# The first weights of seven projections fetched and split in the last turn of the stage before

## The reference

```python
for layer in range(DEPTH):
    h = rmsnorm(x, norm_mix[layer]) * (1 + sc1) + sh1           # both token groups
    y = hyena_mlstm_mixer(...) if layer % 2 == 0 else mla_mixer(...)
    x = x + g1 * y
    x = x + g2 * conv_ffn(rmsnorm(x, norm_ffn[layer]) * (1 + sc2) + sh2, *ffn_p[layer])
x = rmsnorm(x, final_norm)
# second block: one input projection, split by columns
q, k, v, z, xbc, dt_raw, gates = jnp.split(rmsnorm_2(x, norm_mix_w) @ w_in, split_at, axis=-1)
merged = g_attn * (attention @ w_attn_o) + g_ssd * (state_space(z, xbc) @ w_ssd_o)
x = x + merged @ w_out
x = x + hierarchical_moe(rmsnorm_2(x, norm_ffn_w))
```

## Time and profile before

| | |
|---|---|
| median of 3 timed runs | 3491.16 us (3490.48 to 3492.16) |
| the profiled execution | 3485.01 us, span of its instructions 3483.2 us |
| TensorE busy | 3002.3 us, 86% |
| VectorE, ScalarE busy | 1699.8 us (49%), 1214.2 us (35%) |
| mean granted TensorE clock | 0.927 |

### The profile page before, as it was taken

The page is one execution under the profiler, slowest core; times in us unless marked ns, Lnnn a source line. Parts: engine busy times, 40 slices in busy tenths (PEclk is TensorE's granted clock), DMA queues, the critical chain, the costliest instruction groups (busy, mean ns, idle before and its releaser), DMA issues. The chain is left out here.

```text
span 3483.2 us, 38114 instructions
## 1 busy us (share of the span) xinstructions
PE 3002.3 (86%) x14263; PEld 2349.5 (67%) x14263; DVE 1699.8 (49%) x2349; ACT 1214.2 (35%) x1614; POOL 164.8 (5%) x131
## 2 busy tenths in 40 slices
PE   6896788978999999978999999978857788499996
PEld 2382367767888887756777887857635566477775
DVE  1343332354576643424564443341366554488886
ACT  0220022233323232423333442233323322377774
POOL 0000000110001100000000000000000100221210
PEclk9997899899999999989999999989978898699998
DMA  6311011011235333101002221212200013399996
GB/s 244 113 48 64 19 49 49 1 37 73 92 122 169 113 123 100 67 19 45 7 2 96 97 96 68 89 43 85 72 7 1 1 49 146 140 350 350 343 339 241
DMA packets 76311, 362.79 MB, mean 104 GB/s; under 512 B 13428, under 2 KB 17347, under 8 KB 50596
## 3 DMA queue, kind: packets, MB, share of 16 engines
q1 hardware_dynamic: 62404, 327.69, 26.6%
q0 software_dynamic: 13792, 33.58, 2.8%
HBM read 360.68 MB, written 16.27 MB: 108 GB/s over the span
## 5 line engine op out<-in xcount | busy, mean ns | idle before, releaser
L288 PE MATMUL ps<-rounded,rounded 128*128 128x512 f32 (+3 forms) x3700 | 1374.0, 371 | 108.7 <-DVE rounded L1978 24.1
L289 PE MATMUL ps<-rounded,rounded 128*128 128x512 f32 (+3 forms) x3700 | 1334.6, 361 | 0.0
L290 PE MATMUL ps<-rounded,rounded 128*128 128x512 f32 (+3 forms) x3700 | 1332.9, 360 | 0.0
L288 PEld LDWEIGHTS ps<-rounded,rounded 128*128 128x128 f32 (+1 forms) x3700 | 703.8, 190 | 284.8 <-issue 69.5
L290 PEld LDWEIGHTS ps<-rounded,rounded 128*128 128x128 f32 (+1 forms) x3700 | 704.1, 190 | 107.3
L289 PEld LDWEIGHTS ps<-rounded,rounded 128*128 128x128 f32 (+1 forms) x3700 | 705.7, 191 | 95.0
L267 DVE TENSOR_TENSOR rounded<-work,rounded 128x1024 fp32r<-128x1024 f32 (+3 forms) x224 | 306.4, 1370 | 817.5 <-ACT rounded L263 817.0
L263 ACT CAST rounded<-work 128x1024 fp32r<-128x1024 f32 (+3 forms) x224 | 260.8, 1166 | 701.2 <-PE ps L290 561.9
L3125 DVE TENSOR_TENSOR rounded<-work,rounded 128x2048 fp32r<-128x2048 f32 x138 | 311.7, 2288 | 91.1 <-ACT rounded L2973 88.5
L2973 ACT CAST rounded<-work 128x2048 fp32r<-128x2048 f32 x138 | 258.6, 1909 | 83.6 <-PE ps L290 83.6
L274 PE MATMUL ps<-cst 128*128 128x256 f32 x544 | 157.8, 455 | 105.2 <-PEq L169 105.2
(11 more groups left out here) (435 smaller groups left out, 2587.3 us busy)
## 6 DMA issues: line engine op xcount, KB each, us to landing
work<-in_moe SPq DMA_DIRECT2D x138, 1024.0 KB, 7.3
work<-in_ffn_up SPq DMA_DIRECT2D x44, 1024.0 KB, 4.8
work<-in_ffn_down SPq DMA_DIRECT2D x66, 512.0 KB, 3.5
work<-in_ada_w SPq DMA_DIRECT2D x12, 2048.0 KB, 8.6
work<-in_ada_w POOLq DMA_DIRECT2D x48, 512.0 KB, 4.1
work<-in_w_out SPq DMA_DIRECT2D x16, 512.0 KB, 3.5
work<-in_w_gates SPq DMA_DIRECT2D x16, 512.0 KB, 3.6
work<-in_w_in_hy SPq DMA_DIRECT2D x12, 512.0 KB, 3.3
```

What stands on the lines that cost most here:

```text
L288: k.nc.tensor.matmul(out, sh, mh, start=start, stop=False)
L289: k.nc.tensor.matmul(out, sh, ml, start=False, stop=False)
L290: return k.nc.tensor.matmul(out, sl, mh, start=False, stop=stop)
```

## The change

A `Stream` can be made `ahead` of its stage. It then uses one of two sets of semaphores that are not cleared between stages, with a `base` that counts what earlier streams on the set have added. The stage before gets it as `then`: SP issues its first two loads behind its own (`begin`), ScalarE casts tile p right behind the last product that reads slot p and ahead of its evacuation, VectorE subtracts, and the stage itself leaves these steps out. ffn_down's streams get `places` of their own, inside ffn_up's: both raw tiles in ffn_up's raw slot 0, the parts in its raw slot 1 and in the high part of its slot 0. The dummy products at the start of these seven stages go. Seven streams are made ahead: og, ffn_down of block 0 twice and of block 1 once, z, gates, xbc. All other streams pass through the same code with base 0. Left out below are the rest of `project_conv` (SP and VectorE as in `ffn_down` and `ffn_up`, and the dummies only where the stream is not ahead) and `project_act`, edited alike, with `then.low` for both tiles at the end of VectorE's program.

```diff
@@ -235,35 +237,50 @@
 class Stream:
-    def __init__(self, k, name, width, n=2):
-        self.k, self.src, self.n = k, k.dram[name], n
+
+
+    def __init__(self, k, name, width, n=2, ahead=False, places=None):
+        self.k, self.src, self.n, self.ahead = k, k.dram[name], n, ahead
         self.tiles = self.src.shape[0]
         at = MEM - 3 * n * width
         self.at = at - WORK_AT
-        self.raw = [k.words(at + s * width, at + (s + 1) * width) for s in range(n)]
-        spots = [(at + (n + 2 * s) * width, at + (n + 2 * s + 1) * width) for s in range(n)]
+        raw, spots = places or ([at + s * width for s in range(n)],
+                                [(at + (n + 2 * s) * width, at + (n + 2 * s + 1) * width) for s in range(n)])
+        self.raw = [k.words(a, a + width) for a in raw]
         self.parts = [tuple(k.rounded_words(a, a + width) for a in spot) for spot in spots]
         self.high_plain = [high.bitcast(F32) for high, low in self.parts]
-        self.landed, self.rounded, self.ready = ([k.sem(f"{w}{s}") for s in range(n)] for w in ("landed", "rounded", "ready"))
+        self.base = 0
+        if ahead:
+            self.base = sum(other.tiles // n for other in k.ahead[len(k.ahead) % 2::2])
+            self.landed, self.rounded, self.ready = k.ahead_sems[len(k.ahead) % 2]
+            k.ahead.append(self)
+        else:
+            self.landed, self.rounded, self.ready = ([k.sem(f"{w}{s}") for s in range(n)] for w in ("landed", "rounded", "ready"))
         assert self.tiles % n == 0
-    def load(self, sp):
+    def begin(self, sp, before=None):
         for s in range(self.n):
+            if before:
+                sp.wait_ge(before.ready[s], before.base + before.tiles // before.n)
             sp.dma_start(self.raw[s], self.src[s]).then_inc(self.landed[s], 16)
+
+    def load(self, sp, begun=False):
+        if not self.ahead and not begun:
+            self.begin(sp)
         if self.tiles > self.n:
             with sp.Fori(1, self.tiles // self.n) as i:
                 for s in range(self.n):
-                    sp.wait_ge(self.ready[s], i)
+                    sp.wait_ge(self.ready[s], i + self.base)
                     sp.dma_start(self.raw[s], self.src[i * self.n + s]).then_inc(self.landed[s], 16)
     def high(self, act, s, loads):
-        act.wait_ge(self.landed[s], 16 * loads)
+        act.wait_ge(self.landed[s], 16 * loads + 16 * self.base)
         self.k.nc.scalar.copy(self.parts[s][0], self.raw[s]).then_inc(self.rounded[s], 1)
     def low(self, dve, s, loads):
-        dve.wait_ge(self.rounded[s], loads)
+        dve.wait_ge(self.rounded[s], loads + self.base)
         self.k.nc.vector.tensor_tensor(self.parts[s][1], self.raw[s], self.high_plain[s],
                                        ALU.subtract).then_inc(self.ready[s], 1)
@@ -761,6 +780,8 @@
                     act.wait_ge(product[p], i + 1)
                     if not last:
                         stream.high(act, p, i + 2)
+                    elif then:
+                        then.high(act, p, 1)
                     bias = k.col(conv_b, n) if conv_b else 0.0
                     nc.scalar.activation(sums(n, p), k.pair(p)[:, t0:T], ACT.Identity,
                                          scale=k.col(conv_w, n + tiles * (taps // 2)), bias=bias).then_inc(middle, 1)
@@ -823,6 +846,8 @@
         @block.sync
         def _(sp):
             stream.load(sp)
+            sp.wait_ge(stream.ready[0], turns)
+            then.begin(sp)
         @block.tensor
         def _(pe):
@@ -857,6 +882,9 @@
                     act.wait_ge(product[p], i + 1)
                     if not last:
                         stream.high(act, p, i + 2)
+                    else:
+                        act.wait_ge(stream.ready[1], turns)
+                        then.high(act, p, 1)
                     act.wait_ge(taken[p], i + 1)
                     for a, w in segs:
@@ -887,6 +915,8 @@
                     n = 2 * i + p
                     if kind != "last":
                         stream.low(dve, p, i + 2)
+                    else:
+                        then.low(dve, p, 1)
                     dve.wait_ge(middle, ns * (n + 1))
                     for a, w in segs:
                         out = scratch[:, p, a + 1:a + w]
@@ -931,13 +961,14 @@
         @block.sync
         def _(sp):
             stream.load(sp)
+            if then:
+                then.begin(sp, stream)
         @block.tensor
         def _(pe):
-            keep_running(k)
             def turn(i, first, last):
                 for p in range(2):
-                    pe.wait_ge(stream.ready[p], i + 1)
+                    pe.wait_ge(stream.ready[p], i + (stream.base + 1))
                     pe.wait_ge(cut, 2 * i + p + 1)
                     for n in range(DT):
                         done = three_passes(k, k.bank(n, w), [part[:, n * P:(n + 1) * P] for part in stream.parts[p]],
@@ -952,7 +983,8 @@
         @block.scalar
         def _(act):
             def high(n, p, loads):
-                stream.high(act, p, loads)
+                if loads > 1:
+                    stream.high(act, p, loads)
                 nc.scalar.copy(inner.high[:, p, 0:w], hidden[:, n, t0:t0 + w]).then_inc(rounded, 1)
             for p in range(2):
@@ -961,11 +993,16 @@
                 for p in range(2):
                     act.wait_ge(product[p], i + 1)
                     high(2 * i + p + 2, p, i + 2)
+            if then:
+                for p in range(2):
+                    act.wait_ge(product[p], turns)
+                    then.high(act, p, 1)
         @block.vector
         def _(dve):
             def low(n, p, loads):
-                stream.low(dve, p, loads)
+                if loads > 1:
+                    stream.low(dve, p, loads)
                 dve.wait_ge(rounded, n + 1)
                 nc.vector.tensor_tensor(inner.low[:, p, 0:w], hidden[:, n, t0:t0 + w], inner.high_plain[:, p, 0:w],
                                         ALU.subtract).then_inc(cut, 1)
@@ -1378,8 +1425,9 @@
 def mlstm(k, mixed):
     q, key, og = k.area(8 * T, 4, T), k.area(12 * T, 4, T), k.area(16 * T + 6 * 516, 4, T)
     v = k.arena[:, 16 * T:16 * T + 6 * 516].rearrange("p (c h n) -> p c h n", h=ML_HEADS, n=P + 1)
-    project_conv(k, "w_in_qk", k.area(8 * T, 8, T), "ml_conv_w", None, True)
-    project_act(k, "w_in_og", og, ACT.Sigmoid, None, SEGS)
+    w_og = Stream(k, "w_in_og", D, ahead=True)
+    project_conv(k, "w_in_qk", k.area(8 * T, 8, T), "ml_conv_w", None, True, then=w_og)
+    project_act(k, w_og, og, ACT.Sigmoid, None, SEGS)
     project_tokens(k, "w_in_v", v[:, :, :, 0:P], DT, k.h_pair, range(6), ML_W)
     mlstm_core(k, q, key, v, og, k.area(0, 4, T), mixed)
@@ -2615,10 +2663,11 @@
     probs = [k.words(WORK_AT + b * LAT, WORK_AT + (b + 1) * LAT).rearrange("p (c t) -> p c t", t=LAT)
              for b in range(2)]
     load(k, ((cos, "rope_cos"), (sin, "rope_sin")))
-    project_act(k, "w_qk_2", qk, ACT.Identity, None, SEG_LAT, norm=norm)
-    project_act(k, "w_z_2", z, ACT.Silu, None, SEG_LAT)
-    project_act(k, "w_gates_2", gates, ACT.Sigmoid, "b_gate_2", SEG_LAT)
-    project_conv(k, "w_xbc_2", xbc, "conv_w_2", "conv_b_2", True, 7, SEG_LAT)
+    w_z, w_gates, w_xbc = (Stream(k, name, D, ahead=True) for name in ("w_z_2", "w_gates_2", "w_xbc_2"))
+    project_act(k, "w_qk_2", qk, ACT.Identity, None, SEG_LAT, norm=norm, then=w_z)
+    project_act(k, w_z, z, ACT.Silu, None, SEG_LAT, then=w_gates)
+    project_act(k, w_gates, gates, ACT.Sigmoid, "b_gate_2", SEG_LAT, then=w_xbc)
+    project_conv(k, w_xbc, xbc, "conv_w_2", "conv_b_2", True, 7, SEG_LAT)
     project_values(k, v, steps)
     ring = [k.ring[:, j * LAT:(j + 1) * LAT] for j in range(4)]
     normalise_heads(k, qk, lambda n: k.col("qk_norm_2", 0 if n < 4 else 1), ring[0:2], ring[2:4])
@@ -3170,6 +3219,15 @@
     with ExitStack() as ctx:
         k = Kernel(nc, ctx, dram)
+        def ffn(layer, mod, norm, segs, **more):
+
+            at, half = MEM - 6 * 2 * D, 2 * D
+            places = [at, at + D], [(at + half, at + half + D), (at + 2 * half, at + 2 * half + D)]
+            down = [Stream(k, f"ffn_down_{layer}", D, ahead=True, places=places) for seg in segs]
+            ffn_up(k, layer, hidden, scratch, segs, norm, down[0], **more)
+            for n, seg in enumerate(segs):
+                ffn_down(k, down[n], hidden, mod, seg, down[n + 1] if n + 1 < len(segs) else None)
+
         def gain(a):
             return lambda kk, c: k.gain[:, a, kk, c:c + 1]
```

More of the change, by code:

```diff
@@ L732, in _ @@
                 norm.sum_and_spread(pe)
-            else:
+            elif not stream.ahead:
                 keep_running(k)
@@ L752, in _ @@
                 norm.square(act)
-            for p in range(2):
+            for p in range(0 if stream.ahead else 2):
                 stream.high(act, p, 1)
```

49 lines of the change are left out of this document (30 added, 19 removed).

## The result

The changed kernel took 3475.16 us (median of five), the kernel before 3492.16 us in the same comparison: 17 us less. The forecast was 3464.8 us, range 3457 to 3473: the sign is right, the time is 2 us outside the range. Two later comparisons of the same two kernels gave 0.9931 and 0.9914. The 14 runs of the changed kernel have a median of 3470.7 us (3460.7 to 3477.9). The 35 runs of before that stand beside them, on the same three chips, have one of 3493.0: **22.3 us less**, which the expectation of e10 had at 20 to 26.

A forecast was written before the change was run, and what follows sets the result against it. TensorE was taken to set the pace, except at seven starts bound by weight fetch and split. 32.5 - 6.7 - 0.6 + 1.2 = 26.4 us off the profiled 3485.0, plus 6 us for timed runs, gave 3464.8 us, range 3457 to 3473.

The forecast's parts named there:

- Starts, 32.5 us: At the seven stage starts: 48.32 us, minus what cannot be moved, minus lateness from splits in the stage before, saves 32.5 us.
- The lateness of TensorE's first instruction: At og, z, gates and xbc: TensorE's first instruction was assumed 0.05 us after SP's.
- Clock given back, -6.7 - 0.6 + 1.2: Without dummies, og, latent and block 1 lose 6.7 us, the context half 0.6; z wins 1.2, gates and xbc nothing.
- cold starts: At og and the three ffn_down, first real products run at 1.2 GHz, at double length for 3.5 to 5.5 us.
- The rival of the clock that holds: At z, gates and xbc: no low stretch, giving 6.3 instead of 1.2 us, so 3459.7 us; chance 0.17.
- The step that failed is the last one: Whole kernel: 26.4 us off the profiled 3485.0 us, then the same 6 us up to timed runs, giving 3464.8 us.
- The range: Whole kernel: own range 3461 to 3470 us; the clock that holds lowers it to 3457, longer tails raise it to 3473.
- levels of the clock behind later waits: Reason given for the range: these levels fall otherwise when everything is shifted; no size given.
- What would make it wrong: First products waiting for a DMA, a barrier over 3 us later, or stretches outside the seven changing by over 3 us.
- Slower, by the clock: In ffn_down's latent halves TensorE does not regain 2.4 GHz without dummies; 3705 us if both stay at 1.2; chance 0.02.

The follow-up runs named there:

- e10: The changed kernel once more, unchanged, against the kernel before on the same chip: 3467.78 us, ratio 0.9914.
- e8: The fill: changed kernel with dummy products behind the last product of the stage before, except ahead of block 0's latent ffn_down half: 3462.11 us, ratio 0.9894.
- e9: e8 plus dummies around the value projections ahead of block 1's attention (12 instead of 8 at the start, 5 behind the last product): 3450.39 us, ratio 0.9875.
- e15: The same kernel as e9 once more, for its profile and to confirm the time: 3456.55 us, ratio 0.9902 to before.
- e14: Changed kernel with dummies only around the value projections (12 instead of 8 at the start, 5 behind the last product), a repeat: 3462.78 us, ratio 0.9916.
- e6: Changed kernel with only z, gates and xbc begun ahead; og and the three ffn_down start as before, with dummies: 3480.76 us, ratio 0.9945.
- e4: Kernel before with only the dummy products of the seven starts left out, nothing made ahead: 3499.52 us, ratio 1.0027.
- e7: Changed kernel with only og and the three ffn_down begun ahead; z, gates and xbc start as before, with dummies: 3485.86 us, ratio 0.9963.
- e11: The kernel before once more, unchanged, for its profile: 3499.52 us (one run).

## Why the prediction was wrong in its number and right in its parts

- *Starts, 32.5 us*: 32.54 measured. The lateness of TensorE's first instruction was 0.1 to 0.2 us more than assumed at z, gates and xbc (4.92, 5.62 and 5.69 saved, against 5.09, 5.79 and 5.77), made up at the three ffn_down (4.41, 3.09 and 4.11 against 4.27, 2.85 and 3.97).
- *Clock given back, -6.7 - 0.6 + 1.2*: by stretch, means of three profiles of each kernel. Block 0's qk to values 119.24 to 115.08, 4.2 us gained (forecast 3.0); its feed-forward 624.76 to 619.67, 5.1 (3.9); block 1's 418.84 to 419.00, a loss of 0.2 (gain of 1.6); block 2's 248.40 to 230.42, 18.0 (17.9). Sum 27.0 against 26.4. By all seven profiles with these starts it is 3.5, 3.9, 0.5 and 18.1, sum 26.0. That the sums meet so closely is in part luck: of the 4.2 us, 1.0 is chance, as two of the three profiles of before have 3.4 us at 1.2 GHz at the start of qk itself and none of after's has, and the low lengths behind og and the latent half were mis-sized by 1.1 and 1.4 us in opposite directions. That cold starts cost about what was set down is shown by the fill: the clock behind the starts is 1.00, and the stretches are 4.1 us shorter in e8 and 7.3 us on average over e8, e9 and e15. The rival of the clock that holds came true at one start of the three, at gates in after and at xbc in e14 and e6.
- *The step that failed is the last one*: "The timed runs lie 6 us above it, at 3491.2; the same difference gives 3464.8 us". It takes 26.4 us off the median of three timed runs and so puts every change of the clock outside the seven starts at nothing. The runs show that this term is not small: with no edit at all the rest of the span is 2068.8, 2081.6 and 2087.9 us in the three profiles of before, and 2083.4 to 2090.2 in those of after, and single runs of before spread over 26 us. The miss of 10.4 us splits by the medians over the same three chips: 1.8 that the three runs of before (3491.2) lay below 3493.0; 4.1 that the timed gain was 22.3 and not 26.4; 4.5 that the first comparison of after lay above the 3470.7 of all its runs. The profiled execution of before was itself a lucky one, with the lowest rest of 17 profiles. That cancels out of the time forecast, but it is why the two first profiles differ by only 10.8 us.
- *The range* was sized for the cold starts; it named "levels of the clock behind later waits" but gave them no us. Single executions of one kernel spread over 26 us, with the spell in the attention alone worth 7 us or more (195.4 to 201.6 against 186.0 to 188.6), and the stretch from the values of block 2 to its merge takes 276.5, 280.2 and 287.5 us in the three profiles of before. A range of 8 us either way was too narrow for a median of a few runs.
- *What would make it wrong* named "if the stretches outside these seven change by more than 3 us". They did, by 19.5 us between the first two profiles, and by 19.1 us between two of the kernel before as well.
- *Slower, by the clock*: no; block 1's half has 5.0 us at 1.2 GHz behind its start, and its stretch is no longer than before.

The mean rest of after (2087.3) lies 8 us above that of before (2079.4). Of these, 2.8 us come ahead of the first changed stage: qk's weights are issued at 468.6, 469.1 and 467.0 us in before and at 471.9, 471.5 and 469.7 in after, behind the same work. Another 1.9 are in the attention of block 1 and 1.1 between values and merge of block 2. With three profiles each, none of this can be told from chance; the remaining 2 us are open.

## What to carry to other kernels

Weights that are fetched and split in the last turn of the stage before shorten the next start by what a sum over the timeline says, within 0.25 us in each of seven places. Once that is done, dummy products belong behind the last product of a stage, where they fill the evacuation, and not in front of the next, where ready products queue behind them. Before a number is forecast from one profile, compare its granted clock and its long untouched stretches with another profile of the same kernel: a forecast gain of 26 us stands beside a spread of 26 us here. A range for a median of few runs needs a term for that spread.

## What the runs showed of the hardware that was not expected

A TensorE that was busy 9.00 of 9.00 us ran at 1.2 GHz for 24 us on end (five profiles) or 31 us (e4 and e7), behind 1.67 us of idleness, in seven of twelve profiles, in the attention of block 1. At the seven starts of after's first profile the low stretch behind an idle one was 5.0 us at most. The same idle stretch (1.67 us) with the same instructions brought the long spell in some executions and nothing in others: both kernels show both. With 0.30 us in its place it was not seen in five.

The attention is not the only place. Between the values of block 2 and its merge all 17 profiles have a low stretch of 31 to 51 us, with TensorE busy for most of it (46 of 51 us in e11). Where it is 51 us (e8, e10, e11), the way from values to merge takes 286 to 288 us; where none is over 31, 276 to 279. Windows of e11 in it:

```profile
2767.03:2776.03 9.00, 9.00 (x25) 5.51 (x26) 2.08 (x3) 2.66 (x9) 0.00 (x0) 0.50 0.00 0
2776.03:2785.03 9.00, 9.00 (x28) 5.21 (x27) 2.40 (x4) 2.66 (x9) 0.00 (x0) 0.50 0.01 3
```

Idle for 2.8 us, TensorE came back with 3.4 us low at z and xbc and none at gates, in the same execution. In e14, with the same three starts, z was low again, but then gates and not xbc (windows of gates and xbc from their first products):

```profile
2372.75:2379.00 6.25, 6.23 (x21) 5.00 (x22) 0.00 (x0) 0.00 (x0) 0.00 (x0) 0.73 0.53 168
2464.47:2472.00 7.53, 7.53 (x33) 6.27 (x34) 0.00 (x0) 1.71 (x2) 0.00 (x0) 1.00 0.42 139
```

What decides between them was not found. The Trainium skill (TensorE: Matmul & The Clock Gate, Part 1: The HAM clock gate) says that the number of slow matmuls at a kernel's start differs from run to run of the same kernel. The traces here show the same for stretches in the middle, at a price of 7 us or more for the spell in the attention.
